# Turning, routing and experts as one stage in the mixture-of-experts half of two layers

## The chip, the cores and the metric

One core of one Trainium2 chip runs the whole program in one launch. The metric is the device time of that launch in microseconds (us), as the median of several runs.

## The reference

The program takes 512 tokens of width 1024 (float32) through a first block of two layers and then through a second block of two layers. The change concerns only the last part of each layer of the second block, a mixture of 16 experts in 4 groups:

```
x = layer_norm(ALPHA * x + mix, ln1_g, ln1_b)
logits = x @ w_router + router_bias            # 512 x 16
scores = softmax(logits)
group  = argmax over 4 groups of the group's largest score
top_vals, top_idx = top_k(scores in that group, 2)
weights = top_vals / sum(top_vals)
# tokens sorted by expert into blocks of 128 rows
h = silu(xblk @ w_gate[e]) * (xblk @ w_up[e])  # 1024 -> 512
y = h @ w_down[e]                              # 512 -> 1024
x = layer_norm(ALPHA * x + sum of the two weighted y, ln2_g, ln2_b)
```

Both weights of a token are a ratio of two scores of that token, so the softmax's denominator cancels in them, and it does not change which scores are largest.

## The kernel before

The kernel is written in raw blocks: `stage` opens a block in which each engine has its own instruction list and its own semaphores, and closes it with a barrier of all engines. x lies in SBUF as 4 tiles of 128 tokens (`x[:, t, :]`). Large products use three passes over operands that are split into a rounded high part and a low part (`three_passes`, L147): ACT rounds a raw piece into `hi` (L2385), DVE subtracts and leaves the low part in place (`split_piece`, L2484), PE multiplies (L149 to L151).

The last part of `second_layer` (L2577) runs these stages one after the other:

1. `layer_norm_rows` (L493) normalises x. While it runs, its sync queue (SP) also issues `fetch_first_pieces` (L2219): ten pieces of expert weights of 1 MB, six of expert 0 and four of expert 2 of the fixed order.
2. `to_columns` (L418) turns x on PE by 32 transposes with the identity (L431), ACT copies each group of 512 columns out of PSUM (L442) into `xT.hi`.
3. `route` (L1999) loads the router's weights, bias and three small tables (L2031 to L2036), makes the logits as 4 x 8 plain float32 products with a 128x128 tile of x stationary and 16 columns of the router moving (L2043), picks group, first and second expert in a chain of small DVE instructions, each waiting for the one before (`link`, `tt` at L2083), with one Exp on ACT (L2060); ranks of tokens within an expert come from 14 plain products with a triangular table and a table of ones (L2051 to L2054); DVE makes each token's two row numbers (`moe.slot`) and the table of late blocks (`n_late`, `late_expert`, `late_row`). POOL then stores the rows of x by eight indirect DMAs, one per tile and choice, into `x_rows` in DRAM (L2067), and waits for them.
4. `experts` (L2228): a loop (`Fori`) over the late blocks, which always has expert 0's block in it and further ones for experts with more than 128 tokens, then 15 blocks in fixed order. For each block SP loads 128 rows of x (L2265, L2275, L2280, L2289), PE turns them (L2300), ACT rounds (L2390), DVE splits (L2490), PE makes gate and up, ACT silu (L2393), DVE hidden (L2494), PE down, ACT takes the result (L2400), POOL stores it.
5. `combine_experts` (L2552): POOL gathers the expert rows of each token by eight indirect DMAs (L2560), DVE adds them weighted onto x (L2573).
6. `layer_norm_rows` again.

In the loop of `experts` the rounding and splitting of the pieces of a pass stand at its top:

```
for p in GATE + UP + DOWN:
    dve.wait_ge(s.first_rounded, 6 * i + (p + 1))
    split_piece(p, p, s.first_split)
```

The row numbers stand in `moe.slot` token tile first, choice second (column 2t+i); the gathers go in the order of the columns, while DVE adds all four tiles of the first choice and then all four of the second.

## Time and profile before

| what | value |
| --- | --- |
| median of 3 runs | 3622.37 us (3621.12 to 3622.97) |
| the profiled execution's own time | 3624.69 us |
| span of its trace | 3623.0 us |
| granted TensorE clock, mean | 0.896 of full |
| PE / PE weight load | 3018.1 us (83%) / 2402.9 us (66%) |
| DVE / ACT / POOL | 1924.9 (53%) / 1080.0 (30%) / 307.5 (8%) |
| HBM read / written | 413.49 MB / 51.90 MB |

The span runs from the first to the last instruction; what the time has beyond it is launch and end. Busy time is a sum over stages with different limits. PE here is matmul, and "PEld" the weight load beside it; each plain float32 product shows as two records, a turning as one. In the windows of the trace "PEclk" is the granted clock as a share of 2.4 GHz. "DMA share" is the mean busy share of the 16 DMA engines.

### The profile page before, as it was taken

The numbers are of one execution on the slowest core, as the hardware profiler recorded it, in microseconds if no ns is written. First come the engines' busy times: TensorE is split into PE (matmuls) and PEld (weight loads), VectorE is DVE, ScalarE is ACT, GpSimd is POOL, SyncE is SP. The second block draws the span as 40 slices with busy tenths as digits, with TensorE's granted clock in tenths as the row PEclk, the third lists the DMA queues.
The fourth block names the chain that finished last, engine by engine and source line by source line (L and its number), as shares of the span: only waits on it lengthen the run. The fifth ranks groups of instructions, "written<-read, shape, count | busy, mean of one in ns | idle before, by whom it ended". The sixth has DMA issues, their size and how long they took to land. (4 is left out here: it accounts for less than half of the span.)

```text
span 3623.0 us, 35330 instructions
## 1 busy us (share of the span) xinstructions
PE 3018.1 (83%) x13366; PEld 2402.9 (66%) x13366; DVE 1924.9 (53%) x2792; ACT 1080.0 (30%) x1840; POOL 307.5 (8%) x472
## 2 busy tenths in 40 slices
PE   4979988698898798989986499939898998648993
PEld 3757866586776676766875378737676687536882
DVE  3653344342466544655543488744465554347884
ACT  2340130211343112151001277611215100136773
POOL 0020030000342001210000000010121000000001
PEclk8989999789799899989997699969998999769996
DMA  2222202123601131202224399723120222438993
GB/s 84 81 64 82 93 20 82 49 76 113 267 5 53 65 105 58 82 4 70 93 93 153 142 369 405 308 99 105 58 82 4 70 93 93 153 140 313 408 406 125
DMA packets 152240, 467.66 MB, mean 129 GB/s; under 512 B 15598, under 2 KB 29833, under 8 KB 126729
## 3 DMA queue, kind: packets, MB, share of 16 engines
q1 hardware_dynamic: 142712, 431.34, 33.1%
q0 software_dynamic: 9360, 34.08, 2.4%
q8 instruction: 106, 1.74, 0.2%
q14 instruction: 62, 0.50, 0.0%
HBM read 413.49 MB, written 51.90 MB: 128 GB/s over the span
## 5 line engine op out<-in xcount | busy, mean ns | idle before, releaser
L156 DVE CAST weights_r<-weights 128x1024 fp32r<-128x1024 f32 (+4 forms) x270 | 228.6, 847 | 818.5 <-DMA weights<-in_w_in 314.2
L149 PE MATMUL ps<-x_cols_hi_r,weights_r 128*128 128x512 f32 x896 | 361.6, 404 | 48.3 <-DVE weights_r L158 48.3
L158 DVE TENSOR_TENSOR weights_r<-weights,weights_r 128x1024 fp32r<-128x1024 f32 (+4 forms) x270 | 385.9, 1429 | 9.3
L150 PE MATMUL ps<-x_cols_lo_r,weights_r 128*128 128x512 f32 x896 | 357.4, 399 | 0.0
L151 PE MATMUL ps<-x_cols_hi_r,weights_r 128*128 128x512 f32 x896 | 357.1, 399 | 0.0
L149 PEld LDWEIGHTS ps<-x_cols_hi_r,weights_r 128*128 128x128 f32 x896 | 170.4, 190 | 95.2 <-DVE weights_r L158 53.0
L957 POOL TENSOR_SCALAR weights<-weights,weight 128x256 f32<-128x256 f32 (+3 forms) x304 | 151.7, 518 | 728.9 <-DVE weight L851 435.1
L901 ACT ACTIVATE weights<-weights,minus_top 128x256 f32<-128x256 f32 (+3 forms) x304 | 167.0, 551 | 146.9 <-DVE minus_top L814 146.9
L150 PEld LDWEIGHTS ps<-x_cols_lo_r,weights_r 128*128 128x128 f32 x896 | 170.8, 191 | 42.4 <-issue 1.4
L151 PEld LDWEIGHTS ps<-x_cols_hi_r,weights_r 128*128 128x128 f32 x896 | 170.5, 190 | 41.6
L149 PE MATMUL ps<-hawk_xT_hi_r,weights_r 128*128 128x512 f32 x384 | 155.1, 404 | 25.3 <-DVE weights_r L158 25.3
L150 PE MATMUL ps<-hawk_xT_lo_r,weights_r 128*128 128x512 f32 x384 | 153.2, 399 | 0.0
L151 PE MATMUL ps<-hawk_xT_hi_r,weights_r 128*128 128x512 f32 x384 | 152.8, 398 | 0.0
L1936 ACT ACTIVATE sig<-ps 128x512 f32<-128x512 f32 x48 | 28.7, 598 | 406.9 <-PE ps L151 406.9
L149 PE MATMUL ps<-x_cols_hi_r,block_xT_lo_r 128*128 128x512 f32 x264 | 111.5, 422 | 34.0 <-DVE weights_r L2484 30.5
L150 PE MATMUL ps<-weights_r,y_hi_r 128*128 128x512 f32 x320 | 129.1, 403 | 0.0
L151 PE MATMUL ps<-weights_r,y_hi_r 128*128 128x512 f32 x320 | 128.4, 401 | 0.0
L2484 DVE TENSOR_TENSOR raw_pieces_r<-raw_pieces,expert_hi_r 128x2048 fp32r<-128x2048 f32 x46 | 103.3, 2288 | 38.3 <-ACT expert_hi_r L2385 38.3
L149 PE MATMUL ps<-expert_hi_r,hidden_T_lo_r 128*128 128x512 f32 x264 | 107.3, 406 | 7.3 <-DVE hidden_T_lo_r L2497 7.3
L431 PE MATMUL ps<-ident,x 128*128 128x128 f32 x128 | 24.2, 378 | 102.2 <-PEq L89 102.2
L151 PE MATMUL ps<-x_cols_hi_r,block_xT_hi_r 128*128 128x512 f32 x264 | 107.1, 406 | 0.0
L150 PE MATMUL ps<-raw_pieces_r,block_xT_hi_r 128*128 128x512 f32 x272 | 106.9, 393 | 0.0
(475 smaller groups left out, 6902.9 us busy)
## 6 DMA issues: line engine op xcount, KB each, us to landing
weights<-in_w_in SPq DMA_DIRECT2D x64, 1024.0 KB, 5.3
raw_pieces<-in_w_exp_down SPq DMA_DIRECT2D x46, 1024.0 KB, 8.2
raw_pieces<-in_w_exp_up SPq DMA_DIRECT2D x36, 1024.0 KB, 7.6
weights<-in_w_exp_gate SPq DMA_DIRECT2D x34, 1024.0 KB, 7.0
raw_pieces<-in_w_exp_gate SPq DMA_DIRECT2D x32, 1024.0 KB, 7.4
weights<-in_w_exp_up SPq DMA_DIRECT2D x30, 1024.0 KB, 7.4
weights<-in_hawk_w_in SPq DMA_DIRECT2D x28, 1024.0 KB, 5.2
weights<-in_w_exp_down SPq DMA_DIRECT2D x20, 1024.0 KB, 8.2
```

What stands on the lines that cost most here:

```text
L149: pe.matmul(out, as_r(left[1]), as_r(right[0]), start=start, stop=False)
L150: pe.matmul(out, as_r(left[0]), as_r(right[1]), start=False, stop=False)
L151: return pe.matmul(out, as_r(left[0]), as_r(right[0]), start=False, stop=stop)
L156: dve.tensor_copy(as_r(hi), lo).then_inc(rounded, 1)
L158: dve.tensor_tensor(as_r(lo), lo, as_r(hi).bitcast(F32), ALU.subtract).then_inc(done, 1)
L431: mm = pe.transpose(m.ps[:, (k % 8) * BANK + t * P:(k % 8) * BANK + (t + 1) * P], src[:, t, k * P:(k + 1) * P], m.ident[:, :])
L901: act.activation(e(k, p), e(k, p), ACT.Exp, bias=ntop[:, slot, p.stat:p.stat + 1], scale=-1.0, accum_out=total[:, slot, p.stat:p.stat + 1] ...
L957: ins = pool.tensor_scalar(part(p, e(k, p), i), part(p, e(k, p), i), w[:, p.stat + i:p.stat + i + 1], 1.0, ALU.mult, ALU.mult)
L1936: act.activation(sig[:, j, :], m.ps[:, j * BANK:(j + 1) * BANK], ACT.Sigmoid).then_inc(s.gated, 1)
L2484: dve.tensor_tensor(as_r(flat(lo)), flat(lo), as_r(flat(hi[p])).bitcast(F32), ALU.subtract).then_inc(done, 1)
```

## The change

- The router's loads move from `route` into a new `fetch_router`, issued by SP in the layer norm, ahead of the ten expert pieces.
- `to_columns`, `route` and `experts` become one stage, `route_and_run_experts`; there is no barrier between them. SP's load of the first block waits on the stores' semaphore (`copied`); the count of late blocks is waited for by `tabled`.
- PE mixes the turning of x with the logits, two groups behind. The logits have the router's 128x16 piece stationary and 512 tokens moving, in one PSUM bank of 16 rows; ACT copies them out, and four small transposes turn them back.
- Group and expert choice take fewer and wider DVE instructions: a search for the first maximum is four steps (compare, weigh by an order table, maximum, compare) instead of ten; the division of the softmax is gone.
- Ranks are two products of 64 columns (within each tile, and counts of each tile); DVE sums the counts of the earlier tiles.
- Row numbers stand choice first in `moe.slot` (column 4i+t), so the gathers of `combine_experts` come in the order in which DVE adds.
- ACT's rounds and DVE's splits of the first pass's gate and up pieces (4 of 6) move from the loop's top to before the loop; for ACT they come after Exp, for DVE after the late table. Those of the next pass, or of fixed block 1, move to the loop's end. The rooms of the rounded parts are exchanged, since `xT.hi` is still read by the logits.

The core of the diff:

```diff
+    logit_bank, back_bank = m.ps[0:N_EXPERTS, 6 * BANK:7 * BANK], m.ps[:, 7 * BANK:7 * BANK + TT * N_EXPERTS]
+    rank_bank, count_bank = m.ps[:, 0:TT * N_EXPERTS], m.ps[:, BANK:BANK + TT * N_EXPERTS]
...
+        def logits(k):
+            pe.wait_ge(s.col_taken, k + 1)
+            return pe.matmul(logit_bank, c.w[:, k, :], xT[:, k, :], start=k == 0, stop=k == DK - 1)
+
+        for k in range(DK):
+            if k >= 6:
+                pe.wait_ge(s.col_taken, k - 5)
+            for t in range(TT):
+                mm = pe.transpose(m.ps[:, (k % 6) * BANK + t * P:(k % 6) * BANK + (t + 1) * P], x[:, t, k * P:(k + 1) * P], m.ident[:, :])
+            mm.then_inc(s.col_turned, 1)
+            if k == 1:
+                pe.wait_ge(m.router_loaded, c.loaded)
+            if k >= 2:
+                logits(k - 2)
+        logits(DK - 2)
+        logits(DK - 1).then_inc(s.logits_made, 1)
+        pe.wait_ge(s.logits_out, 1)
+        for t in range(TT):
+            mm = pe.transpose(back_bank[:, t * N_EXPERTS:(t + 1) * N_EXPERTS], lgT[:, t * P:(t + 1) * P], m.ident[0:N_EXPERTS, 0:N_EXPERTS])
+        mm.then_inc(s.logits_back, 1)
+        pe.wait_ge(s.chosen, 1)
+        pe.matmul(rank_bank, c.before[:, :], flat(picked[:, :, :]), start=True, stop=True)
+        pe.matmul(count_bank, ones[:, :], flat(picked[:, :, :]), start=True, stop=True).then_inc(s.ranked, 1)
...
+            act.wait_ge(s.col_turned, k + 1)
+            act.activation(xT[:, k, :], m.ps[:, (k % 6) * BANK:(k % 6 + 1) * BANK], ACT.Copy).then_inc(s.col_taken, 1)
+        act.wait_ge(s.logits_made, 1)
+        act.activation(lgT[:, :], logit_bank, ACT.Copy).then_inc(s.logits_out, 1)
+        act.wait_ge(s.centred, 1)
+        act.activation(flat(sc[:, :, :]), flat(lg[:, :, :]), ACT.Exp).then_inc(s.exped, 1)
...
+        def first_of(out, values, top):
+
+            tt(hit[:, :, :], values, spread(top, 4), ALU.is_equal)
+            tt(hit[:, :, :], hit[:, :, :], order[:, :].unsqueeze(1).broadcast_to([P, TT, 4]), ALU.mult)
+            link(dve.tensor_reduce(one_[:, :], hit[:, :, :], AX_X, ALU.max))
+            tt(out, hit[:, :, :], spread(one_[:, :], 4), ALU.is_equal)
...
+        dve.wait_ge(s.exped, 1)
+        link(dve.tensor_reduce(gm[:, :, :], sc[:, :, :].rearrange("p t (g e) -> p t g e", g=G), AX_X, ALU.max))
+        link(dve.tensor_reduce(best[:, :], gm[:, :, :], AX_X, ALU.max))
+        first_of(gsel[:, :, :], gm[:, :, :], best[:, :])
+        tt(tmp[:, :, :].rearrange("p t (e g) -> p t e g", g=G), sc[:, :, :].rearrange("p t (g e) -> p t e g", g=G),
+           gsel[:, :, :].unsqueeze(2).broadcast_to([P, TT, E, G]), ALU.mult)
+        link(dve.tensor_reduce(inside[:, :, :], tmp[:, :, :].rearrange("p t (e g) -> p t e g", g=G), AX_X, ALU.add))
+        first_of(first[:, :, :], inside[:, :, :], best[:, :])
+
+        link(dve.scalar_tensor_tensor(out=tmp[:, :, 0:E], in0=first[:, :, :], scalar=-2.0, in1=inside[:, :, :], op0=ALU.mult, op1=ALU.add))
+        link(dve.tensor_reduce(two[:, :], tmp[:, :, 0:E], AX_X, ALU.max))
+        first_of(second[:, :, :], tmp[:, :, 0:E], two[:, :])
+        for i, chosen in enumerate((first, second)):
+            tt(pick[:, i, :, :].rearrange("p t (g e) -> p t g e", g=G), chosen[:, :, :].unsqueeze(2).broadcast_to([P, TT, G, E]),
+               gsel[:, :, :].unsqueeze(3).broadcast_to([P, TT, G, E]), ALU.mult)
+        dve.tensor_tensor(picked[:, :, :], pick[:, 0, :, :], pick[:, 1, :, :], ALU.add).then_inc(s.chosen, 1)
...
+        dve.wait_ge(s.ranked, 1)
+        counts = by_tile(count_bank)
+        link(dve.tensor_copy(earlier[:, 1, :], counts[:, 0, :]))
+        tt(earlier[:, 2, :], earlier[:, 1, :], counts[:, 1, :], ALU.add)
+        tt(earlier[:, 3, :], earlier[:, 2, :], counts[:, 2, :], ALU.add)
+        tt(cnt[:, :], earlier[:, 3, :], counts[:, 3, :], ALU.add)
+        tt(place[:, :, :], by_tile(rank_bank), earlier[:, :, :], ALU.add)
...
+        tt(chosen_place[:, :, :, :], pick[:, :, :, :], place[:, :, :].unsqueeze(1).broadcast_to([P, 2, TT, N_EXPERTS]), ALU.mult)
+        link(dve.tensor_reduce(slot[:, :, :], chosen_place[:, :, :, :], AX_X, ALU.add))
+        dve.tensor_copy(moe.slot[:, :], flat(slot[:, :, :])).then_inc(s.placed, 1)
+
+        link(dve.tensor_scalar(cnt[:, 0:1], end[:, N_EXPERTS - 1:N_EXPERTS], 1.0, None, ALU.add))
+        dve.tensor_copy(moe.n_late[:, :], cnt[:, 0:1]).then_inc(s.tabled, 1)
...
+def fetch_router(sp, m, a, c):
+
+    sp.dma_start(c.w[:, :, :], a["w_router_2"].rearrange("(k p) n -> p k n", p=P)).then_inc(m.router_loaded, 16)
+    sp.dma_start(c.bias[:, :], a["router_bias_2"].rearrange("(a n) -> a n", a=1).partition_broadcast(P)).then_inc(m.router_loaded, 16)
+    sp.dma_start(c.number[:, :], a["block_number"].partition_broadcast(P)).then_inc(m.router_loaded, 16)
+    for i in range(2):
+        sp.dma_start(c.own[:, i, :], a["own_block"][i:i + 1, :].partition_broadcast(P)).then_inc(m.router_loaded, 16)
+    sp.dma_start(c.before[:, :], a["before"]).then_inc(m.router_loaded, 16)
...
+            sp.wait_ge(s.copied, 16 * 2 * TT)
             sp.dma_start(xe[:, :], rows_at(moe.x_rows, 0)).then_inc(s.first_x_loaded, 16)
...
+            act.wait_ge(m.expert_fetched, 16 * RAW_ROOMS * (layer + 1))
+            for p in GATE + UP:
+                round_piece(p, p, s.first_rounded)
+            late = n_late(act)
             round_x(xT[0], s.first_x_turned, 0, s.first_x_rounded)
             with act.Fori(0, late) as i:
-                def first_round(pieces):
-                    for p in pieces:
-                        act.wait_ge(s.first_loaded[p], 16 * i + 16)
-                        act.wait_ge(s.first_used, 6 * i + (p + 1))
-                        round_piece(p, p, s.first_rounded)
-
-                first_round(GATE + UP)
                 act.wait_ge(s.first_used, 6 * i + 8)
                 silu(s.first_silu_done)
...
+                    act.wait_ge(s.first_loaded[p], 16 * i + 32)
+                    act.wait_ge(s.first_used, 6 * i + (7 + p))
+                    round_piece(p, p, s.first_rounded)
...
+                dve.wait_ge(s.first_rounded, p + 1)
+                split_piece(p, p, s.first_split)
+            late = n_late(dve)
             split_x(xT[0], s.first_x_rounded, 0, s.first_x_split)
             with dve.Fori(0, late) as i:
-                for p in GATE + UP + DOWN:
+                for p in DOWN:
...
+                    dve.wait_ge(s.first_rounded, 6 * i + (7 + p))
+                    split_piece(p, p, s.first_split)
...
-                    dve.wait_ge(s.fetched[2 * t + i], 16)
-                    dve.scalar_tensor_tensor(out=x[:, t, :], in0=rows[:, 2 * t + i, :], scalar=moe.share[:, t, i:i + 1],
+                    dve.wait_ge(s.fetched[i * TT + t], 16)
+                    dve.scalar_tensor_tensor(out=x[:, t, :], in0=rows[:, i * TT + t, :], scalar=moe.share[:, t, i:i + 1],
...
-                        lambda sp: fetch_first_pieces(sp, m, a, layer, raw))
-        to_columns(nc, m, x, TT, [xT.hi[:, k, :] for k in range(DK)])
-        route(nc, m, a, xT.hi, x, moe)
+                        lambda sp: (fetch_router(sp, m, a, router), fetch_first_pieces(sp, m, a, layer, raw)))
         with Tensors(nc) as sb0:
-            hi = [room[:, 4 * half:4 * half + 4, :] for room in (xT.hi, xT.lo, sb0("expert_hi", [P, 8, 512])) for half in range(2)]
-            experts(nc, m, a, layer, moe, raw, hi)
+            hi = [room[:, 4 * half:4 * half + 4, :] for room in (xT.lo, sb0("expert_hi", [P, 8, 512]), xT.hi) for half in range(2)]
+            route_and_run_experts(nc, m, a, layer, x, xT.hi, router, moe, raw, hi)
```

Three places of the program, as instruction orders. The names are those of the program, with PSUM as ps. PE at the routing of a layer, before:

```order
L431 MATMUL ps<-ident,x 128x128 x32
L85 UNCONDITIONAL_BRANCH
L2038 UNCONDITIONAL_BRANCH
L2043 MATMUL ps<-w_router,x_cols_hi 128x16 x32
L2052 MATMUL ps<-picked,before 128x16
L2051 MATMUL ps<-picked,ones 128x16
```

and PE there now:

```order
L2042 MATMUL ps<-ident,x 128x128 x4
L2036 MATMUL ps<-x_cols_hi,w_router 16x512
L2042 MATMUL ps<-ident,x 128x128 x4
L2036 MATMUL ps<-x_cols_hi,w_router 16x512 x3
L2052 MATMUL ps<-ident,logits_T 128x16 x4
L2055 MATMUL ps<-picked,before 128x64
L2056 MATMUL ps<-picked,ones 128x64
```

The 32 short logits products behind the turning have become eight long ones between its groups, and two rank products follow.

DVE from the late table to the first expert block, before:

```order
L2169 TENSOR_SCALAR count<-block_end 128x1
L2170 CAST n_late<-count 128x1
L85 UNCONDITIONAL_BRANCH
L2478 UNCONDITIONAL_BRANCH
L2251 TENSOR_LOAD n_late
L2251 ISA x2
L2490 TENSOR_TENSOR block_xT_lo_r<-ps,block_xT_hi_r 128x512 x2
L2501 UNCONDITIONAL_BRANCH
L2501 ISA
L2484 TENSOR_TENSOR weights_r<-weights,x_cols_hi_r 128x2048
```

and DVE there now:

```order
L2164 MEMSET late_expert 128x1
L2165 MEMSET late_row 128x1
L2494 UNCONDITIONAL_BRANCH
L2498 TENSOR_TENSOR weights_r<-weights,x_cols_lo_r 128x2048 x2
L2498 TENSOR_TENSOR weights_r<-weights,expert_hi_r 128x2048 x2
L2259 TENSOR_LOAD n_late
L2259 ISA x2
L2504 TENSOR_TENSOR block_xT_lo_r<-ps,block_xT_hi_r 128x512 x2
```

Four splits of pieces now stand ahead of the split of the first block's columns.

ACT from Exp into the loop over the late blocks, before (a piece of the difference):

```order
-L2060 ACT_TABLE_LOAD
-L2060 ACTIVATE scores<-logits 128x64
-L85 UNCONDITIONAL_BRANCH
-L2380 UNCONDITIONAL_BRANCH
-L2251 TENSOR_LOAD n_late
-L2251 ISA x2
-L2390 ACTIVATE block_xT_hi_r<-ps 128x512 x2
-L2403 UNCONDITIONAL_BRANCH
```

and now:

```order
+L2066 ACT_TABLE_LOAD
+L2066 ACTIVATE scores<-logits 128x64
+L2396 UNCONDITIONAL_BRANCH
+L2399 ACTIVATE x_cols_lo_r<-weights 128x2048 x2
+L2399 ACTIVATE expert_hi_r<-weights 128x2048 x2
+L2259 TENSOR_LOAD n_late
+L2259 ISA x2
+L2404 ACTIVATE block_xT_hi_r<-ps 128x512 x2
+L2421 UNCONDITIONAL_BRANCH
+L2421 ISA
+L2407 ACT_TABLE_LOAD
+L2407 ACTIVATE silu<-ps 128x512
```

The four rounds stand behind Exp, and the first activation in the loop is silu.

## Rows read from the trace of the kernel before

**Rows 1.** The page's busy tenths of PE in 40 slices.

```profile
PE   4979988698898798989986499939898998648993
```

**Rows 2.** Windows, layer one: stretch, length, busy PE, PEld, DVE, ACT, POOL, PEclk, DMA, GB/s.

```profile
1966.90:1971.00 4.10, 4.08 (x19) 4.10 (x20) 0.00 (x0) 2.18 (x4) 0.00 (x0) 0.50 1.01 420
1971.00:1982.30 11.30, 1.60 (x15) 1.36 (x14) 0.17 (x1) 3.55 (x6) 0.00 (x0) 0.80 0.83 312
1982.30:1996.20 13.90, 13.83 (x64) 13.72 (x64) 0.00 (x0) 0.00 (x0) 0.00 (x0) 0.50 0.00 0
1996.20:2008.20 12.00, 0.00 (x0) 0.00 (x0) 9.55 (x56) 0.26 (x1) 0.00 (x0) 0.50 0.00 1
2008.20:2014.50 6.30, 6.16 (x28) 6.05 (x28) 0.68 (x5) 0.00 (x0) 0.00 (x0) 0.50 0.00 0
2014.50:2018.50 4.00, 0.00 (x0) 0.00 (x0) 3.34 (x17) 0.00 (x0) 0.00 (x1) 0.50 0.00 0
2018.50:2031.60 13.10, 0.00 (x0) 0.00 (x0) 1.43 (x10) 0.00 (x0) 7.86 (x8) 0.50 0.81 320
2031.60:2034.90 3.30, 0.00 (x0) 0.00 (x0) 0.00 (x0) 0.00 (x0) 0.00 (x0) 0.50 0.01 2
2034.90:2038.10 3.20, 0.00 (x0) 0.00 (x0) 0.00 (x0) 0.00 (x0) 0.00 (x0) 0.50 0.50 164
2038.10:2046.30 8.20, 1.97 (x8) 1.57 (x8) 3.70 (x4) 6.74 (x6) 0.00 (x0) 0.50 0.19 64
```

**Rows 3.** Timeline at the logits, layer one: start us, us, engine, line, operation.

```profile
1974.05 0.38 SPq L2031 DMA_DIRECT2D w_router<-in_w_router  x1
...
1982.29 13.84 PE L2043 MATMUL ps<-w_router,x_cols_hi 128*128 128x16 f32 x64 [9.70 <-DMA before<-in_before]
```

**Rows 4.** Timeline of PE at the rotation products.

```profile
1428.05 3.60 PE L354 MATMUL ps<-q_lo,rotate 128*128 128x512 f32 x8
```

**Rows 5.** Windows at the products with eight stationary columns (columns as in rows 2).

```profile
1641.00:1644.00 3.00, 3.00 (x6) 0.52 (x5) 0.00 (x0) 2.98 (x5) 0.00 (x0) 0.61 1.04 359
1644.00:1647.00 3.00, 3.00 (x9) 0.63 (x8) 2.75 (x2) 0.07 (x1) 0.00 (x0) 1.00 0.61 238
```

**Rows 6.** Timeline of DVE in the choice.

```profile
1998.08 0.22 DVE L2107 TENSOR_REDUCE group_top<-scores 128x16 f32<-128x64 f32 x1
1998.34 0.17 DVE L2108 TENSOR_REDUCE best<-group_top 128x4 f32<-128x16 f32 x1
1998.54 0.17 DVE L2083 TENSOR_TENSOR hit<-group_top,best 128x16 f32<-128x16 f32 x1
```

**Rows 7.** Groups of POOL, 2000 to 2400 us: busy us, mean ns, idle before.

```profile
L2067 POOL DMA_INDIRECT expert_x_rows<-x,slot x8 | 7.9, 983 | 381.8 <-DVEq L2156 379.7 <-issue 2.1
```

**Rows 8.** Timeline from the first block's columns to the first expert matmul.

```profile
2040.76 0.69 DVE L2490 TENSOR_TENSOR block_xT_lo_r<-ps,block_xT_hi_r 128x512 fp32r<-128x512 f32 x1 [0.16 <-ACT block_xT_hi_r L2390]
...
2043.98 4.49 DVE L2484 TENSOR_TENSOR weights_r<-weights,x_cols_hi_r 128x2048 fp32r<-128x2048 f32 x2 [2.53 <-ACT x_cols_hi_r L2385]
...
2046.32 0.79 PE L149 MATMUL ps<-x_cols_hi_r,block_xT_lo_r 128*128 128x512 f32 x1 [6.23 <-DVE weights_r L2484]
```

**Rows 9.** Timeline of the combination, layer one.

```profile
2373.20 1.28 DVE L2573 SCALAR_TENSOR_TENSOR x<-expert_rows,share,x 128x1024 f32<-128x1024 f32 x1 [3.02 <-DMA expert_rows<-expert_y_rows,slot]
2373.80 1.49 POOL L2560 DMA_INDIRECT expert_rows<-expert_y_rows,slot  x1 [0.30 <-issue]
...
2383.38 6.07 DVE L2573 SCALAR_TENSOR_TENSOR x<-expert_rows,share,x 128x1024 f32<-128x1024 f32 x5 [1.75 <-DMA expert_rows<-expert_y_rows,slot]
```

**Rows 10.** Timeline of ACT in the late loop, layer two.

```profile
3248.28 1.08 ACT L2400 ACTIVATE block_y<-ps 128x512 f32<-128x512 f32 x2 [7.08 <-PE ps L151]
3249.39 1.28 ACT L2385 ACT_TABLE_LOAD   x1
...
3279.11 1.08 ACT L2400 ACTIVATE block_y<-ps 128x512 f32<-128x512 f32 x2 [7.02 <-PE ps L151]
```

**Rows 11.** Windows behind the last gather, layer one (columns as in rows 2).

```profile
2384.00:2386.00 2.00, 0.00 (x0) 0.00 (x0) 2.00 (x3) 0.00 (x0) 0.00 (x0) 0.50 0.01 2
```

267 lines of the change are left out of this document (104 added, 163 removed).

## The prediction

> **What bounds the kernel now.** First the page: TensorE is busy 83% of the span, but its weight loads only 66%, and the granted clock averages 0.896, so some stretches are not matmul work. The strip of 40 slices of 90.6 us [rows 1] shows holes in PE: the 23rd and 36th slice, near 1995 and 3180 us, hold the routing of tokens to experts, the 27th and the last the combination and layer norm, once per layer each. The chain that ended last tells only of the last layer norm, so I read the stretches directly. [rows 2] cut the first hole into pieces that follow one another; their sum, 79.4 us, is the time from the first turning product of x (1966.9) to the first expert matmul (2046.32). No two pieces overlap: columns of x, router loads, logits, choice on DVE, ranks on PE, places on DVE, eight row stores from POOL, a stage change, a load of rows back, then turning and weight preparation. In each, one engine or one transfer is the bound and the others wait. The second layer's hole has the same pieces (the strip), and I count both alike. So a cut anywhere on this chain is a cut of the span, unless something else is late there.
>
> **The logits.** Now: 4.1 us of turning at clock 0.50, then faster [rows 2], then the router loads, issued at 1974.05 behind ten expert pieces, end PE's wait at 1982.29; 64 short matmul records take 13.84 us [rows 3]; DVE starts at 1996.2. From 1966.9 that is 29.3. After: the router's loads are ahead of the pieces, a layer norm earlier, so the 8.3 us between turning's end and logits go, and the logits are eight products with 512 moving columns, two records each. A plain fp32 record of that size takes 3.60/8 = 0.45 at full clock with its tail, 0.43 paced [rows 4]; with a narrow stationary (8 columns) six start in 3 us at 0.61 and nine at 1.00 [rows 5], so the narrowness buys nothing. I take 0.86 per product at full clock, 1.71 at half. Turning groups of four take some 0.85 at half clock (19 products in 4.1 us, [rows 2]) and half that after. PE: three groups (2.6) and one product (1.7) until about 4.2, where the clock rose before too; then five groups (2.1) and seven products (6.0), 0.2 tail: 12.5. ACT's copy of the 16x512 result 0.6 and two handoffs, four small turnings back 0.8: DVE starts at 14.2 instead of 29.3. **Gain 15.1.** If the clock stayed at half as in the old logits: 22.3, gain 7.0.
>
> The pieces now queue behind small router transfers. Their issue took SP some 5 us before; they are needed by ACT at about +15 (after Exp) and by DVE at +27. Both kinds had landed by 1982.3, +15.4 [rows 3]; five more is +20, and ACT, faster per piece than DVE, still has seven us of lead for its first. I cost this at nothing; its cover is the routing itself.
>
> **The choice.** Now 56 DVE instructions in 12.0 us [rows 2]. Dependent steps follow each other every 0.20 us with 16 columns, every 0.26 with 64 [rows 6]. After: up to Exp and back 1.1 as now; then group maximum and best 0.46, three searches of four steps 0.8 each, two wide steps and two narrow ones 0.93, two picks and their sum 0.75: 5.64. **Gain 6.2.** The last sum signals by itself, not by a further instruction.
>
> **The ranks.** Now 28 records, 6.3 us [rows 2], after four records of 64 columns. The nearest row is the old pace, 6.16/28 = 0.22 (floor 0.9); with four times the columns at half clock no more than 0.41 (ceiling 1.6). I take 1.2 plus 0.2 of handoff. **Gain 4.9.** Places: 17 steps instead of 16, two of them 128 columns wide, 3.9 instead of 3.65; POOL starts 0.05 sooner. **Loss 0.2.** The table for the late blocks, some 2.0 us of DVE, stays beside the stores.
>
> **The stores.** Eight on POOL at (7.9+2.1)/8 = 1.25 us [rows 7]; transfers take (2031.6-2020)/8 = 1.45 each and queue behind one another, so data end 13.4 after the places are known. Here the change adds a rival on SBUF. Four splits of 2.2 us [rows 8] now run on DVE from +2.0 to +10.9 after the places, beside POOL's issues. Such an overlap stands in the last stage: POOL's indirect DMA at 2373.80, begun under a DVE instruction that ends at 2374.48, takes 1.49 [rows 9], against a mean of 0.98 of the stores [rows 7]; it waits for about the rest of the DVE instruction. Walking this through: POOL's first two are free, numbers three to six each wait for a split to end and so start 2.2 apart, seven and eight are free again. The last issue ends 3.9 later, but the transfers then have no queue, and data end at +16.25: **loss 2.85**. The bounds: no loss, or POOL held until the fourth split ends, 7.4.
> The Trainium skill, "SBUF — State Buffer", section "Who interferes with whom", says that a VectorE instruction with two SBUF inputs blocks a GpSimd instruction that reads SBUF, which agrees with [rows 9]; the same section infers that tensor_tensor leaves descriptor generation alone, and by that the loss would be nothing (5.7 us less in all).
>
> **The stage change.** From the end of the data to SP's load of the first block 3.3 us [rows 2]; after, SP waits on the stores themselves. How long the completion takes in this is not shown: between 0.5 (the same load's data end to PE's start) and 2.0. I take 1.0 and 0.1 for SP: **gain 2.2** (1.3 to 2.8). Load and turning, 3.2 and 3.3, stay.
>
> **Prepared pieces.** Now DVE has the block's columns split at 2041.45, but the first expert matmul starts at 2046.32, waiting for a table load, a round and a split [rows 8]. After, those were done 6 us and more before. **Gain 4.8.** What is late next is the row load itself; the splits' only cost is the one above. From PE's start on the loop runs as before: silu, the down pieces and hidden keep their distances, since their order on ACT and DVE is unchanged.
>
> **The loop's end.** ACT loads a table before the rounds at each pass's head (1.28, [rows 10]); now silu is first there, its table loading while PE works. On the path this counts where a second pass follows, once, in layer two: **gain 1.3**.
>
> **The combination.** POOL gathers in the order in which DVE now reads. Before, DVE took the fourth first choice at 2383.38 and then had five instructions back to back until 2389.45 [rows 9], though the last gather's data had ended by 2384.0 [rows 11]. After, one instruction of 1.28 follows the last landing (2384.5): 2385.8. Between one instruction's lag more and none, 2.4 to 3.6; I take **3.4**, in each layer. Later waits of POOL behind DVE lie under queued transfers.
>
> **Sum.** Per layer 15.1 + 6.2 + 4.9 - 0.2 - 2.85 + 2.2 + 4.8 = 30.2, and 3.4: 33.6; two layers 67.2, and 1.3: 68.5. The profiled execution took 3624.69 (span 3623.0), so its like would take 3556.2; the median of the three runs is 2.3 lower: **3554 us**.
>
> **Rivals.**
> Half clock through the logits: PE is busy all through the old logits, yet at 0.50 [rows 2]. Against it: 512-column products with 8 stationary columns rose to 1.00 [rows 5]. Price 8.1 per layer: 3570. Chance 0.10.
> The stores aren't slowed by the splits: the overlap in [rows 9] is with a scalar_tensor_tensor with both inputs in SBUF, the splits are tensor_tensor, and only under the former does the trace show a gather. 2.85 x 2 = 5.7 less: 3548. Chance 0.25. (The Trainium skill's "SBUF — State Buffer" infers this case, as cited above.)
> POOL gets no turn until all splits are done: (7.4-2.85) x 2 = 9.1 more: 3563. Against it: in the combination POOL got in after one instruction; but there DVE wasn't queued up behind. Chance 0.12.
> The cuts don't meet: pieces so late behind the router loads, or the gathers so slow, that about a third of 68.5 is not had: 3577. The slack above speaks against it. Chance 0.04.
> Slower: the logits are summed in another order; a token near a tie could change its expert and fill one block more. A pass of the late loop costs 3279.11-3248.28 = 30.8 us [rows 10]. It decides from the third further pass on (92.4 against 68.5): 3646. One or two would leave 3585 or 3616. Nothing in the trace says that a count is near its edge. Chance 0.02 for all, of which slower 0.01.
> The forecast itself, 0.47.
>
> **Range.** The cases from 3548 to 3563 hold 0.84; with their unknown prices (completion 1.7 up or down in all, ranks 0.8, combination 2, searches 2) and part of the half-clock case, 3543 to 3570. Sizes below 0.2%, 7 us, can't be told from no change by a measurement of this kernel; the forecast is 1.9%. Faster 0.97, same 0.01, slower 0.02.
>
> **What would show it.** In the changed profile: turning's first product to DVE's first logits step 14 us, with the clock at 1.00 from about 4 us on; 28 DVE instructions there in under 6 us; ranks under 1.5; POOL's middle stores near 1.9 us each while splits run (0.95 throughout would be the second rival, one of 8 or more the third); SP's load within 1.5 us of the last store's data; PE's first expert matmul right behind the split of the columns; one instruction after the last gather. The forecast is wrong if 1966.9 to the first expert matmul doesn't come down from 79.4 to 46 to 52, or if the experts' static blocks change their length.

## The result

The changed kernel takes **3566.78 us** (median of 4 runs, 3564.81 to 3573.93) where the kernel before took 3622.67 in the same session: ratio 0.9849, interval 0.9832 to 0.9866, or 55.9 us less. The forecast was 3554, range 3543 to 3570. So sign and range held, and the gain came out 12.6 us smaller than the 68.5 forecast.

The page of the changed kernel, its PE strip beside [rows 1]; a slice is 89.3 us here. The two holes of the routing, slices 22 and 23 and slices 35 and 36, are shallower (7 4 and 6 5 tenths, where [rows 1] has 6 4 both times), and the clock in slices 23 and 36 is still at 0.6 and 0.7:

```profile
PE   4979988699798797999997499939799999658993
...
PEclk8989999799699898989998699969898999879997
```

Layer one's routing in the changed kernel, in stretches that follow one another as in [rows 2] (columns: busy time of PE, PEld, DVE, ACT, POOL, granted clock, DMA share, GB/s). They are: turning at half clock; turning and logits at full clock; the choice; the ranks; the places; the stores; SP's issue and the load of the block's rows; its turning and split.

```profile
1973.06:1977.60 4.54, 4.54 (x14) 2.52 (x14) 0.51 (x6) 1.79 (x3) 0.00 (x0) 0.50 1.02 426
1977.60:1988.41 10.81, 9.99 (x39) 3.40 (x38) 0.00 (x0) 4.16 (x7) 0.00 (x0) 0.99 1.00 414
1988.41:1994.14 5.73, 0.00 (x0) 0.00 (x0) 4.65 (x25) 4.79 (x5) 0.00 (x0) 0.76 0.03 13
1994.14:1995.60 1.46, 1.11 (x4) 0.93 (x4) 0.75 (x5) 1.46 (x1) 0.00 (x0) 0.50 0.00 0
1995.60:1999.36 3.76, 0.00 (x0) 0.00 (x0) 3.22 (x17) 2.01 (x2) 0.00 (x0) 0.50 0.00 0
1999.36:2016.80 17.44, 0.00 (x0) 0.00 (x0) 10.07 (x14) 0.00 (x0) 12.40 (x8) 0.50 0.60 241
2016.80:2020.48 3.68, 0.00 (x0) 0.00 (x1) 0.00 (x0) 0.00 (x0) 0.00 (x0) 0.50 0.39 142
2020.48:2023.95 3.47, 1.97 (x9) 1.58 (x9) 1.38 (x2) 2.04 (x3) 0.00 (x0) 0.50 0.11 19
```

The sum is 50.9 us where it was 79.4. Turning and logits, 15.35, took 29.3 before; the choice 5.73 instead of 12; ranks and places 5.2 instead of 10.3. But the stores now take 17.4, and DMA is busy for only 60% of them: POOL hands the work out too slowly. Its issues, and the splits on DVE beside them:

```profile
1999.66 1.19 POOL L2073 DMA_INDIRECT expert_x_rows<-x,slot  x1 [354.36 <-DVE n_late L2154]
...
2000.71 2.29 DVE L2498 TENSOR_TENSOR weights_r<-weights,x_cols_lo_r 128x2048 fp32r<-128x2048 f32 x1
...
2001.15 2.68 POOL L2073 DMA_INDIRECT expert_x_rows<-x,slot  x1 [0.30 <-issue]
2002.91 2.28 DVE L2498 TENSOR_TENSOR weights_r<-weights,x_cols_lo_r 128x2048 fp32r<-128x2048 f32 x1
2004.13 1.89 POOL L2073 DMA_INDIRECT expert_x_rows<-x,slot  x1 [0.30 <-issue]
...
2008.53 1.90 POOL L2073 DMA_INDIRECT expert_x_rows<-x,slot  x1 [0.30 <-issue]
2010.73 0.95 POOL L2073 DMA_INDIRECT expert_x_rows<-x,slot  x1 [0.30 <-issue]
```

An issue takes 0.95 alone and 1.89 to 2.68 beside a split (up to 2.78 in layer two). Numbers two to five are held; the third starts 2.98 behind the second, and the next three follow 2.20 apart. In [rows 7] the mean was 0.98 and they were 1.25 apart.

All kernels of this study can be compared by stretches (e1 to e12 are the experiments below; "the places" are each token's two row numbers). They run from the first turning product to DVE's first logits step; from the places (end of the last cast of the slots) to the end of POOL's last issue, to SP's load, to the first expert matmul; from there to the first silu and to the first gather; from the first gather's issue to DVE's last product of the combination. In the last column stands everything from layer one's first turning product to the end of the span. Values of layer one / layer two from each kernel's one profile:

| kernel | logits | last issue | load | first matmul | its silu | gather | combination | to the end |
|---|---|---|---|---|---|---|---|---|
| before | 29.3 / 29.5 | 10.35 / 10.22 | 16.7 / 16.4 | 28.2 / 27.9 | 7.32 / 7.29 | 321.9 / 352.9 | 21.2 / 20.9 | 1656.1 |
| changed | 15.4 / 15.4 | 14.8 / 14.8 | 18.0 / 18.0 | 24.6 / 24.7 | 8.13 / 8.11 | 325.2 / 355.5 | 18.3 / 16.9 | 1598.8 |
| e1 | 15.1 / 15.3 | 14.8 / 14.8 | 18.0 / 18.0 | 24.6 / 24.7 | 7.96 / 8.10 | 326.4 / 355.5 | 16.9 / 17.6 | 1599.0 |
| e2 | 15.3 / 15.3 | 14.8 / 14.8 | 18.0 / 18.0 | 24.7 / 24.6 | 8.08 / 8.09 | 325.0 / 355.4 | 18.0 / 17.4 | 1599.6 |
| e3 | 15.3 / 15.2 | 12.9 / 12.9 | 16.5 / 16.5 | 23.3 / 23.3 | 7.16 / 8.58 | 324.9 / 354.9 | 17.6 / 17.9 | 1595.2 |
| e4 | 14.6 / 14.9 | 10.4 / 10.4 | 14.0 / 14.1 | 20.7 / 20.8 | 7.96 / 8.02 | 326.6 / 356.9 | 17.3 / 17.0 | 1588.8 |
| e5 | 15.7 / 16.1 | 14.8 / 14.8 | 18.0 / 18.0 | 24.7 / 24.7 | 8.08 / 8.14 | 325.1 / 355.5 | 18.4 / 17.1 | 1613.1 |
| e6 | 29.3 / 29.6 | 10.4 / 10.3 | 16.8 / 16.4 | 28.3 / 27.8 | 8.59 / 7.42 | 320.8 / 353.3 | 17.0 / 17.5 | 1648.9 |
| e7 | 15.3 / 15.4 | 14.8 / 14.8 | 18.0 / 18.0 | 24.7 / 24.9 | 8.01 / 8.03 | 324.2 / 354.4 | 18.0 / 16.9 | 1597.8 |
| e8 | 15.3 / 15.4 | 14.0 / 14.0 | 17.1 / 17.1 | 23.9 / 23.9 | 8.43 / 8.47 | 325.9 / 354.7 | 17.7 / 17.1 | 1597.4 |
| e9 | 15.3 / 14.9 | 10.9 / 11.0 | 14.5 / 14.5 | 21.2 / 21.2 | 8.10 / 7.88 | 324.2 / 354.1 | 18.0 / 16.8 | 1587.7 |
| e10 | 14.8 / 14.6 | 10.4 / 10.4 | 14.0 / 14.1 | 20.0 / 20.1 | 5.85 / 5.87 | 322.1 / 351.7 | 18.5 / 17.0 | 1590.8 |
| e11 | 29.2 / 29.5 | 10.3 / 10.2 | 16.8 / 16.4 | 28.2 / 27.9 | 7.36 / 7.34 | 322.1 / 353.2 | 20.9 / 20.7 | 1656.1 |
| e12 | 15.4 / 15.2 | 10.4 / 10.9 | 14.0 / 14.5 | 20.1 / 20.5 | 5.86 / 5.86 | 322.0 / 351.8 | 17.6 / 17.3 | 1581.4 |

So from the first turning product on the change brings 57 us in both profiles of it. From the first expert matmul to the first gather it is *longer* by 3.3 and 4.5 us in layer one, 2.6 in layer two. That was forecast as unchanged or 1.3 shorter.

### The profile page after: what moved, and what is told of

It reads as the page before. It is cut to its first block and busy times, and to the rows that moved or that the text cites. A ratio compares the mean times of both kernels' runs of the same rounds, so it can differ in the third digit from the quotient of the medians.

```text
span 3571.9 us, 34899 instructions
## 1 busy us (share of the span) xinstructions
PE 3015.2 (84%) x13230; PEld 2378.2 (67%) x13230; DVE 1916.7 (54%) x2740; ACT 1077.2 (30%) x1839; POOL 316.4 (9%) x472
## 5 line engine op out<-in xcount | busy, mean ns | idle before, releaser
L1936 ACT ACTIVATE sig<-ps 128x512 f32<-128x512 f32 x48 | 28.7, 598 | 406.9 <-PE ps L151 406.9
L2498 DVE TENSOR_TENSOR raw_pieces_r<-raw_pieces,x_cols_hi_r 128x2048 fp32r<-128x2048 f32 x46 | 103.4, 2289 | 54.5 <-ACT x_cols_hi_r L2399 54.5
L149 PE MATMUL ps<-x_cols_lo_r,block_xT_lo_r 128*128 128x512 f32 x264 | 113.1, 428 | 22.4 <-DVE weights_r L2498 15.9
L149 PE MATMUL ps<-x_cols_hi_r,hidden_T_lo_r 128*128 128x512 f32 x264 | 107.8, 408 | 7.3 <-DVE hidden_T_lo_r L2511 7.3
L151 PE MATMUL ps<-x_cols_lo_r,block_xT_hi_r 128*128 128x512 f32 x264 | 108.7, 412 | 0.0
L151 PE MATMUL ps<-x_cols_hi_r,hidden_T_hi_r 128*128 128x512 f32 x264 | 106.3, 402 | 0.0
```

The source lines that it names most:

```text
L149: pe.matmul(out, as_r(left[1]), as_r(right[0]), start=start, stop=False)
L151: return pe.matmul(out, as_r(left[0]), as_r(right[0]), start=False, stop=stop)
L1936: act.activation(sig[:, j, :], m.ps[:, j * BANK:(j + 1) * BANK], ACT.Sigmoid).then_inc(s.gated, 1)
L2498: dve.tensor_tensor(as_r(flat(lo)), flat(lo), as_r(flat(hi[p])).bitcast(F32), ALU.subtract).then_inc(done, 1)
```

## The experiments

### Once more

e1, no edit.

> The changed kernel once more, unedited. Its profiled execution lay 7 us above the median of its timed runs, and 6.6 us of its distance to the kernel before had arisen ahead of the changed stages, in the first block's attention stages near 880 to 1170 us, whose code is the same. If that is scatter, this profile shows the first changed stage (the first turning product of x) again 0 to 2 us from where it begins in the kernel before (1966.9), and the time is 3564 to 3567. If it is a lasting effect of the new program (other addresses, other code), it shows it at 1972 to 1974 again, and the time of the profiled run is 3570 or more.

Measured: 3565.48, 3566.49, 3576.34, 3574.59, 3569.44, median 3569.44; before in the same session 3626.64; ratio 0.9845 (0.9831 to 0.986). The profiled run is the 3565.48 and has the first turning product at 1964.5, 2.4 us *ahead* of the kernel before. In the first profile it lay at 1973.06, 6.1 behind. So that lag was scatter, not an effect of the change. Over all profiles of the study but that with the router's loads last, this point lies between 1964.1 and 1975.5, whatever the kernel. It goes with the clock: ahead of this product e6 spends 344.5 us at 0.50 and reaches it at 1964.1, e11, whose code is the same up to there, 364.6 us and 1975.5. How a late rise of the clock costs time shows layer two's attention, in two kernels with the same code there. First the kernel with extra products (e10 below), which reaches this point 8.8 us earlier, then the one with both mends (e9):

```profile
2740.00:2745.00 5.00, 5.00 (x16) 3.58 (x15) 2.04 (x10) 2.59 (x9) 1.16 (x3) 0.50 0.00 0
2745.00:2751.00 6.00, 6.00 (x22) 4.07 (x21) 3.42 (x12) 1.39 (x5) 0.00 (x0) 0.69 0.01 3
2751.00:2760.00 9.00, 9.00 (x54) 6.87 (x52) 7.08 (x29) 6.64 (x24) 2.06 (x4) 1.00 0.00 1
```

```profile
2733.00:2738.00 5.00, 5.00 (x20) 4.20 (x18) 1.41 (x8) 3.12 (x9) 2.06 (x4) 0.50 0.00 0
2738.00:2743.00 5.00, 5.00 (x17) 3.12 (x17) 3.25 (x7) 1.41 (x6) 0.00 (x0) 0.73 0.02 3
2743.00:2748.00 5.00, 5.00 (x30) 3.77 (x29) 3.64 (x17) 4.57 (x16) 2.07 (x4) 1.00 0.00 0
```

PE is busy without a pause in both. By the windows' means the clock rises at about 2748.7 in the first and 2740.7 in the second; with the 8.8 us by which the first is ahead, that is 16.8 us more at half clock, or about 8.4 us of time. At the same instruction near 2754 the first is only 1.0 ahead, so 7.8 are lost. But e10 is the exception here: this stretch at half clock lasts 47.8 us in its profile, 27.3 in e4's and 34.1 in the other twelve. Why it was long there is open, and that the extra products had a part in it is not ruled out. In general a run is some us longer or shorter by where the clock rises in the attention stages. This is why kernels are compared by stretches, and whole runs only by medians.

### The splits beside the stores

Three edits to the changed kernel and a variant of the third. The first, e2:

```
+        pool.sem_inc(s.issued, 1)            # behind the eight stores
...
+            dve.wait_ge(s.issued, 1)
             for p in GATE + UP:
```

> All four early splits wait until POOL has issued its eight row stores. Theory: under a split an issue on POOL takes 1.9 instead of 0.95, one turn per split. Then all eight are 0.95 here, 1.25 apart, the last ends 9.8 after the places (now 14.8), the data end 13.4 after them (now 17.4), SP's load follows 0.6 later, the columns' split would be ready 20.5 after the places, and the four splits end at 19.2 after them, so the first expert matmul starts 20.9 after the places instead of 24.6: 3.7 less per layer, 7.4 in all, a time near 3559. Rival: the issues are slow for another reason (the queue of descriptors is full with transfers): then they stay at 1.9, the splits only come later (done 24 after the places), and the time rises by 0 to 8.

Measured: 3566.72 (3564.47 to 3570.91), and the first matmul 24.7 after the places, as in the changed kernel. Neither theory was tested, since nothing was held: DVE's first split begins while POOL is at its first issue, and the issues are as long as in the changed kernel.

```profile
1991.39 1.19 POOL L2073 DMA_INDIRECT expert_x_rows<-x,slot  x1 [354.24 <-DVE n_late L2155]
...
1992.43 2.29 DVE L2499 TENSOR_TENSOR weights_r<-weights,x_cols_lo_r 128x2048 fp32r<-128x2048 f32 x1
...
1992.88 2.68 POOL L2073 DMA_INDIRECT expert_x_rows<-x,slot  x1 [0.30 <-issue]
```

The increment that stands behind eight indirect DMAs in POOL's program arrived before the second of them had been issued. So here the increment did not say that the indirect DMAs ahead of it had been issued.

The second edit, e3, has the same wait, and so in effect only a move: two of the four splits go behind the split of the block's columns.

```
-            for p in GATE + UP:
+            dve.wait_ge(s.issued, 1)
+            for p in GATE:
...
             split_x(xT[0], s.first_x_rounded, 0, s.first_x_split)
+            for p in UP:
+                dve.wait_ge(s.first_rounded, p + 1)
+                split_piece(p, p, s.first_split)
```

> The two gate splits wait for POOL's last issue, the two up splits follow the split of the block's columns. Theory as in the run before it: the two are done 14.6 after the places, so nothing stands before the columns' split, ready at 20.5; first expert matmul 20.6 after the places, 4 less than now, 8 in all, if PE's gate products (two pieces) cover the two up splits (4.6 us) and the down splits behind them: a time near 3559. If the late up splits are on the path instead, some 2 to 5 us per layer come back and it is slower than the run before it. Rival (issues slow for another reason): no gain, 3566 or more.

Measured: 3561.65 (3559.95 to 3563.88), ratio 0.9816 (0.9801 to 0.9831). With two splits beside them instead of four, two issues are held instead of four, the last one ends 12.9 after the places instead of 14.8, and the first matmul comes 1.3 to 1.4 sooner per layer (4 were expected: two splits still hold two issues). Two splits less gave 1.9 us of issues, or 0.95 each: that is an issue's extra time. The rival of a full queue ("no gain, 3566 or more") did not come. The splits behind show no wait of PE from its first expert product to the silu.

The third, e4, leaves the splits where they are and cuts each in four:

```
-                split_piece(p, p, s.first_split)
+                for q in range(4):
+                    part = slice(512 * q, 512 * q + 512)
+                    low, high = flat(raw[p])[:, part], flat(hi[p])[:, part]
+                    ins = dve.tensor_tensor(as_r(low), low, as_r(high).bitcast(F32), ALU.subtract)
+                ins.then_inc(s.first_split, 1)
```

> Each early split as four DVE instructions of a quarter of the columns (some 0.6 us each), in the same place as now. If POOL waits for the instruction that DVE has begun and then gets its turn, an issue is held by no more than 0.6: 1.2 to 1.6 each, starts some 1.75 apart, last end 12.8 after the places instead of 14.8, so 2 less per layer and 4 in all: 3563. If POOL got its turn only where DVE really pauses, it would now come no sooner than behind all sixteen: 3567 to 3575. If it is the amount of DVE traffic that counts and not the instruction's length, nothing changes: 3567.

Measured: 3561.09 (3556.61 to 3563.56), ratio 0.9816 (0.9801 to 0.9831), better than expected. The issues are nearly as fast as with no split beside them (the second takes 1.08 and 1.19, the third to eighth 0.95):

```profile
1995.75 1.08 POOL L2073 DMA_INDIRECT expert_x_rows<-x,slot  x1 [0.30 <-issue]
1995.92 4.46 DVE L2519 TENSOR_TENSOR weights_r<-weights,x_cols_lo_r 128x512 fp32r<-128x512 f32 x7
1997.14 0.95 POOL L2073 DMA_INDIRECT expert_x_rows<-x,slot  x1 [0.30 <-issue]
...
2000.30 5.05 DVE L2519 TENSOR_TENSOR weights_r<-weights,expert_hi_r 128x512 fp32r<-128x512 f32 x8
...
2003.42 0.95 POOL L2073 DMA_INDIRECT expert_x_rows<-x,slot  x1 [0.30 <-issue]
```

The last issue ends at 10.4 (before: 10.35), the load is issued at 14.0, the first matmul is at 20.7 instead of 24.6. So what the whole splits cost is **3.95 us in layer one** (3.9 in layer two), and it is the length of one DVE instruction that costs, not the traffic: the sixteen short ones read and write the same bytes. Nor is it a queue full of transfers, the rival of e2 and e3: the same transfers are issued without a wait here. Halves (e8), by the same code with `range(2)` and 1024 columns:

> Each early split as two DVE instructions of half the columns, 1.15 us each, between the change's whole ones (2.29 us: five issues held, POOL 14.8 us from the places to the last issue) and the quarters (none held, 10.4). If an issue waits for the instruction that DVE has begun whenever it comes to one, halves hold it by up to 1.15: issues of 1.0 to 2.0, last end 11.5 to 13.5. If an issue has a part of its own, some 0.9 long, in which DVE may go on unseen, halves cost at most 0.3 each: last end 10.5 to 11.5. If the length does not count but the number of instructions, the last end is nearer to 14.8.

```profile
1997.46 1.61 POOL L2073 DMA_INDIRECT expert_x_rows<-x,slot  x1 [0.30 <-issue]
1998.16 3.49 DVE L2519 TENSOR_TENSOR weights_r<-weights,x_cols_lo_r 128x1024 fp32r<-128x1024 f32 x3
1999.38 1.96 POOL L2073 DMA_INDIRECT expert_x_rows<-x,slot  x1 [0.30 <-issue]
2001.56 4.62 DVE L2519 TENSOR_TENSOR weights_r<-weights,expert_hi_r 128x1024 fp32r<-128x1024 f32 x4
2001.64 1.97 POOL L2073 DMA_INDIRECT expert_x_rows<-x,slot  x1 [0.30 <-issue]
...
2006.18 0.95 POOL L2073 DMA_INDIRECT expert_x_rows<-x,slot  x1 [0.30 <-issue]
```

Measured: 3571.34 (2 runs, too few to tell it from the changed kernel), last issue at 14.0: beyond the figures of the first two theories. The third's figure is near, but its reason, the number of instructions, is refuted by the quarters. The held issues start 2.27 apart. Half splits start 1.13 apart here ((2001.56 - 1998.16)/3), so that is two of them, as 2.20 is one whole split.

The rows show what paces them. Each held issue, beside wholes and halves, ends 0.82 to 0.84 us after the end of the DVE instruction that was running when the issue began (2004.13 + 1.89 = 2006.02 against a split's end at 2005.19), and the gather of [rows 9] 0.81 after it (2375.29 against 2374.48). So an issue waits for the DVE instruction in progress and then needs some 0.8 us more. Quarters are a near tie: left alone they start 0.60 apart, so two are 1.20, and an undisturbed issue recurs every 1.25; a quarter and an issue then begin within 0.02 us of each other. In e4 the quarter gives way each time, by 0.05, and from the third issue on none waits. In both layers of e9 and in layer two of e12, with the same splits, one issue waits instead:

```profile
2004.42 1.49 POOL L2073 DMA_INDIRECT expert_x_rows<-x,slot  x1 [0.30 <-issue]
2006.22 0.95 POOL L2073 DMA_INDIRECT expert_x_rows<-x,slot  x1 [0.30 <-issue]
```

There the last issue ends at 10.95 instead of 10.4. So quarters are free or cost 0.5 us, by how the two engines happen to meet, and halves save only 0.8 of the 4.4. Other lengths weren't tried.

### The order of the loads

e5 changes one line:

```
-                        lambda sp: (fetch_router(sp, m, a, router), fetch_first_pieces(sp, m, a, layer, raw)))
+                        lambda sp: (fetch_first_pieces(sp, m, a, layer, raw), fetch_router(sp, m, a, router)))
```

> The changed kernel, with the router's loads issued behind the ten expert pieces again (both still in the layer norm's stage). If transfers come in the order of their issue, the router's weights land after the pieces, some 15 to 17 us after the first turning product, and the eight products start only then: DVE has the logits at 24 to 26 instead of 15.2, and the kernel is 17 to 22 us slower than the changed one, 3584 to 3590. If small transfers get past the large ones, the logits stay at 15 to 17 and the time at 3565 to 3570: then the order of the loads was worth nothing.

Measured: 3598.67 (3594.98 to 3600.91), ratio 0.9919 (0.9904 to 0.9934): 29 to 32 us slower than the changed kernel, half more than expected, and in another place. The logits are at 15.7 and 16.1 after the first turning product, nearly as in the changed kernel. What got longer is the layer norm ahead. SP's own rows in it:

```profile
1959.33 2.11 SPq L2216 DMA_DIRECT2D w_router<-in_w_router  x1
1961.48 17.57 SPq L2217 DMA_DIRECT2D router_bias<-in_router_bias  x1
...
1981.32 0.43 SPq L2221 DMA_DIRECT2D before<-in_before  x1
```

SP hangs for 17.57 us in issuing the load of the router's bias (0.58 in the changed kernel, where it is ahead of the pieces). The stage ends when SP is through, at 1981.75, and the turning starts at 1982.63, though x was normalized at 1969.4. So this load behind ten queued pieces (1 MB each) isn't only late itself: its issue holds SP, and with it the stage that waits for SP. The forecast put the router's loads ahead of the pieces and costed what that does to the pieces at nothing, which held; it did not see that the other order costs some 15 us per layer.

### The gathers alone

e6 is the kernel before, with the slots in the order first choices, second choices:

```
-        slot = sb("slot", [P, TT, 2])
+        slot = sb("slot", [P, 2, TT])
...
-                    dve.wait_ge(s.fetched[2 * t + i], 16)
+                    dve.wait_ge(s.fetched[i * TT + t], 16)
```

> The kernel before, with the new order of slots alone: stores as before, but the gathers of the combination come in the order in which DVE reads them. The forecast's term: 3.4 less per layer, 6.8 in all. From the first gather's issue to DVE's last instruction it took 21.2 and 20.9 us in the kernel before, and 16.9 and 17.6 in the changed one; so here 17 to 18, and a time 6 to 8 below the kernel before. The rival: the changed kernel's gathers also start 1.2 us later behind the last store of results, and the blocks lengthen by 0.08 each; if both come from this part, the gain here is only 1 to 3.

Measured: 3622.45 (10 runs, 3614.62 to 3625.4) beside 3626.89 (15 runs), ratio 0.9987 (0.9977 to 0.9996), 4.4 us less. By the stretches the combination is 4.2 and 3.4 us shorter, as in the changed kernel, and the stretch to the end is 7.2 shorter; the runs' interval, 1.5 to 8.3 us, holds both this and less. The part does what it says. The gathers do not start later here (6.19 and 6.56 us behind the last store of results, as in the kernel before), and the static blocks keep their length. Both belong to the other parts of the change.

### What the experts' stage lost

From the first silu on, the time of each block's silu shows how the stretch grows: against the kernel before the first is 0.6 to 0.8 late, then each of the 15 static blocks adds 0.06 to 0.08 (18.07 us from silu to silu, where it was 18.00), then the last block and the stage change add more. The edit for the blocks, e7, puts the router's tensors behind the rooms of the pieces:

```
+        raw_rooms = [*m.w_slots] + [sb("raw_pieces", [P, 8, 512]) for _ in range(RAW_ROOMS // 2 - 2)]
         router = bag(w=sb("w_router", [P, DK, N_EXPERTS]), bias=sb("router_bias", [P, N_EXPERTS]), before=sb("before", [P, P]),
                      number=sb("block_number", [P, MAX_BLOCKS]), own=sb("own_block", [P, 2, N_EXPERTS]), loaded=96 * (layer + 1))
-        raw_rooms = [*m.w_slots] + [sb("raw_pieces", [P, 8, 512]) for _ in range(RAW_ROOMS // 2 - 2)]
```

> The changed kernel with the router's tensors allocated behind the rooms of the raw pieces, so that these stand at their old addresses. In the static blocks TensorE is busy without a pause, 18.05 us per block before, 18.13 now, and products that read the raw pieces take 396 ns instead of 389. If the address does it, the blocks are back at 18.05 and both layers together 2.2 us shorter than the changed kernel; if it is something else in the new stage (the order of the rounded rooms, other waits), the blocks stay at 18.13.

Six static blocks of layer one, kernel before, changed kernel (its second profile), and this one, grouped (count, then busy time and mean ns of one):

```profile
L150 PE MATMUL ps<-raw_pieces_r,block_xT_hi_r 128*128 128x512 f32 x56 | 21.8, 389 | 0.0
```
```profile
L150 PE MATMUL ps<-raw_pieces_r,block_xT_hi_r 128*128 128x512 f32 x56 | 22.2, 396 | 0.0
```
```profile
L150 PE MATMUL ps<-raw_pieces_r,block_xT_hi_r 128*128 128x512 f32 x56 | 21.9, 391 | 0.0
```

Measured: from the third static block on, the silus keep their distance to those of the kernel before (0.99 to 1.03 late in layer one, 0.95 to 1.06 in layer two), so the growth per block is gone, 0.8 us in layer one and 1.15 in layer two. The same products take 389 ns in the kernel before, 396 on tiles at the new addresses, and 391 back at the old ones. In the runs (3568.17, 3563.28 to 3576.29) so small a thing is not to be seen.

The stage change at the end: from the last store of results to DVE's first instruction of the combination 5.46 and 5.86 us before, 6.66 and 6.28 in the changed kernel and nearly the same in all its variants (6.60 to 6.68, 6.27 to 6.30). e11 tests one cause of it. Before, then changed:

```profile
2362.05 0.53 POOL L2548 DMA_DIRECT2D expert_y_rows<-block_y  x1 [17.03 <-ACT block_y L2400]
2367.51 1.90 DVE L2566 TENSOR_SCALAR x<-x 128x1024 f32<-128x1024 f32 x3 [14.23 <-PEq L89]
```
```profile
2341.80 0.53 POOL L2567 DMA_DIRECT2D expert_y_rows<-block_y  x1 [16.89 <-ACT block_y L2414]
2348.46 1.90 DVE L2585 TENSOR_SCALAR x<-x 128x1024 f32<-128x1024 f32 x3 [15.29 <-PEq L89]
```

> The kernel before with 13 more signals in the experts' stage, which nobody uses: as many as the change moved into it. From the last store of results to DVE's first instruction of the combination it takes 5.46 us (layer one) and 5.86 (layer two) in the kernel before, 6.66 and 6.28 in the changed one. If the clearing of the signals at the stage's end is what grew, it is near 6.7 and 6.3 here too. If not, it stays at 5.5 and 5.9, and the growth comes from the code of the stage or its place in memory.

Measured (one run, 3633.28): 5.56 and 5.95. The signals cost 0.1, not 1.2 and 0.4. What made this change longer is open.

The rest is the clock. Windows of the first expert products before, and in the changed kernel (its second profile):

```profile
2046.00:2048.00 2.00, 1.68 (x4) 1.39 (x5) 2.00 (x2) 2.00 (x2) 0.00 (x0) 0.50 0.03 8
2048.00:2050.00 2.00, 2.00 (x7) 1.52 (x7) 2.00 (x2) 1.98 (x2) 0.00 (x0) 0.62 0.00 0
2050.00:2052.00 2.00, 2.00 (x10) 1.65 (x9) 2.00 (x2) 0.65 (x1) 0.00 (x0) 1.00 0.12 16
```
```profile
2015.00:2017.00 2.00, 1.82 (x4) 1.49 (x5) 0.04 (x1) 0.62 (x1) 0.00 (x0) 0.50 0.70 252
2017.00:2019.00 2.00, 2.00 (x6) 1.56 (x5) 0.00 (x0) 0.00 (x0) 0.00 (x0) 0.50 0.00 0
2019.00:2021.00 2.00, 2.00 (x8) 1.59 (x8) 0.00 (x0) 0.00 (x0) 0.00 (x0) 0.81 0.00 0
```

PE begins at 2046.32 and at 2015.18. The clock is at 0.50 for 3.2 us of work before and for 4.6 after. It rose 3.1 to 3.4 us behind the first expert product in five of the six layers with the old stage (before, e6, e11) and 6.0 behind it in one; with the new stage it was 4.4 to 5.0 in fourteen of eighteen layers and 2.8 to 6.0 in the four of e3 and e8 (e10 and e12 left out). What sets the moment is open. The same in layer two's second pass of the late loop: from the taking of the result to PE's next product 6.69 us before and 5.26 in the changed kernel, so the table load really went (1.43, forecast 1.3); but from that product to the silu it is 7.18 before and 8.16 now: the clock rises 2.9 us behind the product before and 5.0 now.

### Both mends, and TensorE kept busy

e9 is the quarters and the old addresses together:

> Quarters for the early splits and the raw pieces at their old addresses, together. The quarters alone took 3.95 us per layer from the stretch between the places and the first expert matmul (24.64 to 20.7) and the old addresses 0.8 and 1.1 us from the static blocks. The places are apart, so they should add: 9.8 us less than the changed kernel in all, 3557 to 3559. If the median is not below that of the quarters alone (3561), the addresses are worth less than runs scatter.

Measured: 3556.01 (3552.49 to 3564.74), ratio 0.9799 (0.9785 to 0.9812), against 0.9849 and 0.9845 of the changed kernel: 11 to 13 us less by medians, 11 by the stretch to the end, where 9.8 were expected. They add; but the quarters alone brought only 3.5 per layer here (24.65 to 21.2), since one issue was held in each, as shown above, so the rest of the 11 holds some scatter beside the addresses' 2.

Then, in e10 and e12, products whose result nobody reads:

```
         pe.matmul(count_bank, ones[:, :], flat(picked[:, :, :]), start=True, stop=True).then_inc(s.ranked, 1)
+        pe.wait_ge(s.placed, 1)
+        for n in range(16):
+            pe.matmul(m.ps[:, 7 * BANK:8 * BANK], m.ident[:, :], x[:, n % TT, 0:512], start=True, stop=True)
...
+        @block.tensor                        # in the layer norm, not in e12
+        def _(pe):
+            for n in range(68 if warm is not None else 0):
+                pe.matmul(m.ps[:, 7 * BANK:8 * BANK], as_r(warm[:, n % DK, 0:P]), as_r(warm[:, n % DK, :]), start=True, stop=True)
```

> The kernel with both, and TensorE kept busy where it waits: 68 products into a bank that nobody reads while the layer norm runs, 16 plain fp32 products of 512 columns between the places and the load of the block's rows. The output is the same. Theory: the half clock at the start of the turning (4.6 us of work at 0.50) and at the first expert matmul (some 4 us at 0.50) is due to TensorE's pause before it; with work there the granted clock is 1.00 when they start, DVE has the logits at 13.0 instead of 15.2, the first silu comes 2 us earlier behind the first expert matmul, and the turning of the block 0.5 earlier: 4 to 5 us per layer, 8 to 10 in all, 3548 to 3552. Rivals: the short pauses that remain (the stage change, the load) bring the clock down again, then 0 to 2 us in all; or the extra products run over into the work that waits for TensorE, then it is slower by what they overrun, up to 3 us per layer.

Measured: 3562.02 (3548.29 to 3562.84), ratio 0.9805 (0.9788 to 0.9822), no gain in whole runs. By stretches the two places differ. In the layer norm, then stage change, then turning:

```profile
1965.00:1968.00 3.00, 2.83 (x13) 2.02 (x11) 3.00 (x4) 0.00 (x0) 0.00 (x0) 1.00 1.02 431
1968.00:1970.00 2.00, 0.04 (x1) 0.07 (x2) 1.23 (x2) 0.00 (x0) 0.00 (x0) 1.00 1.02 430
1970.00:1973.00 3.00, 3.00 (x14) 1.97 (x14) 0.51 (x6) 1.79 (x3) 0.00 (x0) 0.59 1.00 421
```

PE held 1.00 to the end of the extra products and was at 0.59 in the first 3 us behind a pause of 2: only 0.5 us won (0.3 in layer two). At the stores it worked: clock 1.00 at the first expert product, which comes 20.0 after the places, and the silu 5.86 behind it instead of 8.1. The profile also has the late rise of the clock in layer two's attention that is shown above, 8 us, which hides the gain in this run: 1590.8 to the end, where e9 has 1587.7. Whether the other runs of e10 have it too is not recorded; no profile of another kernel has it, so that the 68 products bring it is not ruled out. So the last run, e12, keeps only the 16 products:

> Both mends (quarters, old addresses) and of the extra products only the 16 during the row stores, since the clock fell again in the stage change behind the layer norm (0.59 over the first 3 us of the turning) while at the stores it stayed at 1.00. Expected by stretches, since whole runs scatter by 10 us with the clock of the attention stages: the first expert matmul 20.0 us after the places (21.2 without the extra products), the first silu 5.9 behind it (8.0), so 3.2 less per layer and 6.4 in all against the kernel with both mends; from the first turning product to the span's end 1581 instead of 1587.7, and a median of 3547 to 3556. If the extra products bring a lower clock later on, as a whole or in the next attention stage, the second layer's attention is longer and the median stays at 3556 or more.

```profile
2018.00:2022.00 4.00, 4.00 (x18) 3.25 (x19) 0.00 (x0) 0.26 (x1) 0.00 (x0) 1.00 0.27 104
```

Measured: **3550.67** (3544.72 to 3558.33), ratio 0.9795 (0.978 to 0.9811), and 1581.4 from the first turning product to the end, on the 1581 expected. It is the fastest version of the study by its median. Its interval overlaps that of e9, so that it beats e9 rests on the stretches (6.3 us), not on the ratios; some 0.5 us of these is the issue that was held in layer one of e9 and not here. Layer two's attention has 34.1 us at half clock here, not e10's 47.8.

## Why the prediction was right, and where it was off

The gain came where the forecast put it, in the chain of the routing and in the combination, and its terms hold to about 1 us each but for the stretch that was to stay as it was. That the time lies inside the range is in part luck: the range's upper part stood for half clock through the logits and for POOL held by all splits, which did not come, while the loss in the experts' stage had no term. e3, e4 and e8 test the term of the stores, e5 the order of the loads, e6 the combination and e7 the static blocks; logits, choice, ranks and prepared pieces have no run of their own and are read from the stretches. By its own steps, per layer, in the second profile of the changed kernel against the kernel before:

- **Logits**, forecast 15.1: 14.2 and 14.1. The clock rose 4.1 and 4.6 us behind the first turning product (forecast 4.2). Off was the pace behind it: a group of turning and a product start 1.55 apart, where 0.42 and 0.86 had been taken. The rows have 0.59 for the turning and 0.96 for the product between turnings, 0.92 in a row at the end.
- **Choice** 6.2, **ranks and places** 4.7: 6.2 and 4.8. Counting dependent steps by 0.20, 0.26 and so on, from [rows 6], came out: 5.7 long where 5.64 was counted. (12.0 less 5.64 is 6.36; the forecast wrote 6.2.)
- **Stores** and **stage change**, forecast -2.85 and +2.2: together -1.2 and -1.6 instead of -0.65. The mechanism was the right one, one turn per split, and the rival by which tensor_tensor leaves POOL alone is refuted by the changed kernel's issues and by e3 and e4. The size was off: numbers two to five were held, not three to six, the second for 2.68, so that the last issue ended at 14.8, 4.4 later than with quarters (forecast 3.9), and with the data's end at 17.4 instead of 16.25 it all costs 3.95. The stage change gained more than forecast, since SP's load follows the data by 0.6 (forecast 1.1).
- **Prepared pieces** 4.8: 4.8 (load to first matmul 11.5 before, 6.65 now).
- **Routing** in all 30.2 forecast, 28.7 and 28.35 measured, and 50.7 to 51.0 us long where "46 to 52" was to show it.
- **Combination** 3.4: 4.3 and 3.3; e6 has it alone.
- **Loop's end** 1.3, and **static blocks unchanged**: this is the step that failed, and by the prediction's own words ("or if the experts' static blocks change their length") a sign of it being wrong, from 18.00 to 18.07 us a block. The stretch from the first expert matmul to the first gather was to be 1.3 shorter in all and is 7.1 longer. By the silus, both layers together: 1.5 from the clock that rises later behind the first expert product, 0.6 in the late loop and its end (there the clock gives back 1.0 of the 1.4 of the table load), 2.0 from the pieces' addresses, 1.65 from the longer stage change, whose cause is open, and 1.4 from layer one's last block, 25.9 us from its silu to its last store instead of 24.4. This last comes and goes: the first profile has 24.4 in both layers, and e6, whose experts' stage is the old one, has 25.3 in one. It is not shown to come from the change.

The sum: 57.1 from routing, 7.5 from the combination, less 7.1 lost in the experts and 0.4 elsewhere, give the 57.1 of the last column; with the forecast's 60.4, 6.8 and 1.3 the shortfall is 11.4: 3.3 in the routing, 8.4 in the experts, less 0.7 for the combination, and 0.4 elsewhere. Half clock through the logits did not come, nor did POOL wait for all splits; no further late pass was needed (two in layer two, one in layer one, as before).

The Trainium skill, "SBUF — State Buffer", section "Who interferes with whom", infers that tensor_tensor does not hold descriptor generation: it takes only the read interface of the pair that VectorE and GpSimd share, and descriptor generation needs the write interface. The traces of this case do not agree: an indirect DMA's issue takes 1.9 to 2.7 us instead of 0.95 beside tensor_tensor instructions of 2048 columns, 1.6 to 2.0 beside those of 1024, and 0.95, at times 1.49, beside quarters.

## What to carry to other kernels

Before work is put beside POOL's DMA issues, see how long one of its DVE instructions is against the issue's own period of 1.25 us: whole splits of 2.20 cost 4 us per layer, halves still 3, quarters 0 to 0.5. Small loads belong ahead of large ones even where they have time, since the issue itself can block its engine and through it a stage. And a forecast should not carry "the rest stays as it is" at nothing: an earlier start can meet a lower clock, and moved tensors can change the pace of a stage that nobody touched.

## What the runs showed of the hardware that was not expected

- An increment placed behind eight indirect DMAs in POOL's program arrived before the second was issued.
- SP needed 17.57 us to issue one small load behind ten queued pieces; 0.58 ahead of them.
- An indirect DMA's issue on POOL that begins under a DVE instruction with two SBUF inputs ends 0.8 us after that instruction: DVE starts 2.20 and 1.13 apart gave issues 2.20 and 2.27 apart. With DVE starts 0.60 apart either DVE gave way by 0.05 or POOL waited 0.54.
- Products with the moving operand at another place in SBUF took 396 instead of 389 ns, in a stage where PE never waits.
- With PE busy without a pause, the same attention stage had the clock at 0.50 for 27.3 to 47.8 us in fourteen executions; and the first turning product lay anywhere in 11 us, by how long the clock was at 0.50 ahead of it (344.5 against 364.6 us at the two ends). That scatter is larger than most of the effects measured here.
